# A trunk kernel: first two weight groups in pieces of 272, 384 and 448 columns, work moved between engines at the start, and another order at the end

## The reference, cut to what matters

```python
q, k, v, g, gg, pv, pg, fq, fk, fv, logf, fg = split(rmsnorm(h, norm_pre) @ w_in)   # 1024 -> 3222 columns
g = log_sigmoid(glr @ w_up + b_gate) / 16          # forget gate, from the 16 low-rank columns glr
o_gla  = chunked gated linear attention(q, k, v, g)
o_pool = (trailing means of pv - pv) @ pool_w * pool_scale
o_fox  = forgetting softmax attention(fq, fk, fv, cumsum(logf)), for the samples over the cache too
y = concat(rmsnorm(o_gla) * silu(gg), o_pool * silu(pg), o_fox * silu(fg)) @ w_out
h = h + rmsnorm(y, norm_post)
```

## Time and profile before

| what | value |
|---|---|
| median of 3 runs | 712.42 us (710.39 to 712.92) |
| the profiled execution | 712.99 us, span 711.3 us |
| TensorE busy | 667.0 us of the span (94%) |
| VectorE, ScalarE, GpSimd busy | 389.3, 256.9, 140.0 us |
| first matmul of weight group 2 | at 48.22 us |
| first matmul of the output projection | at 604.30 us |
| last matmul | at 702.97 us |

### The profile page before, as it was taken

One profiled execution on the slowest core, in us unless ns is written; L12 is line 12 of the kernel. 1 busy time (PEld: TensorE's weight loads), 2 busy tenths in 40 slices (PEclk: granted clock), 3 DMA queues, 4 the chain that ended last, 5 costly groups with the idle time before them and its releaser, 6 DMA issues.

```text
span 711.3 us, 13069 instructions
## 1 busy us (share of the span) xinstructions
PE 667.0 (94%) x5120; PEld 565.3 (79%) x5120; DVE 389.3 (55%) x706; ACT 256.9 (36%) x453; POOL 140.0 (20%) x161
## 2 busy tenths in 40 slices
PE   2999999999999999999999989999899887999995
PEld 2799999888999989999999945666576654688884
DVE  4824926572455305169999956345433549245433
ACT  6637343111111256122121154644564557221221
POOL 3034112111111011233222130223222102112210
PEclk9999999999999999999999999999999999999999
DMA  8412103131001032352210480557665502032232
GB/s 245 121 38 54 36 1 73 32 89 30 7 27 30 5 83 91 100 168 72 59 30 1 138 272 3 176 180 212 185 214 176 208 32 103 1 105 96 82 119 89
DMA packets 60758, 67.28 MB, mean 95 GB/s; under 512 B 15188, under 2 KB 50907, under 8 KB 60697
## 3 DMA queue, kind: packets, MB, share of 16 engines
q1 hardware_dynamic: 55529, 51.37, 24.4%
q0 software_dynamic: 5168, 15.08, 6.8%
HBM read 57.71 MB, written 8.68 MB: 93 GB/s over the span
## 4 chain that ended last, share of the span: by engine, by line
PE 66%; DVE 20%; issue 4%; ACT 4%; SPq 3%; DMA 2%; DVEq 0%; ACTq 0%
PE PS L1743 9%; PE PS L1744 8%; PE PS L1745 8%; DVE RA L1412 7%; PE PS L1672 5%; PE PS L1671 5%; PE PS L1673 5%; PE PS L2032 3%; PE PS L1989 3%; PE PS L1967 3%; PE PS L2014 2%; PE PS L1932 2%; PE PS L1919 2%; DVE wr L1241 2%; DVE PT L1611 1%
## 5 line engine op out<-in xcount | busy, mean ns | idle before, releaser
L1743 PE MATMUL PS<-xh,wh 128*128 128x368 f32 x576 | 196.6, 341 | 0.9 <-DVE RA L1372 0.6
L1744 PE MATMUL PS<-xl,wh 128*128 128x368 f32 x576 | 190.5, 331 | 0.0
L1745 PE MATMUL PS<-xh,wl 128*128 128x368 f32 x576 | 190.0, 330 | 0.0
L568 POOL TENSOR_TENSOR wl<-wr,wh 128x1024 fp32r<-128x1024 f32 x24 | 61.7, 2570 | 298.0 <-ACT wh L929 298.0
L1743 PEld LDWEIGHTS PS<-xh,wh 128*128 128x128 f32 x576 | 108.5, 188 | 5.2 <-issue 2.5
L1744 PEld LDWEIGHTS PS<-xl,wh 128*128 128x128 f32 x576 | 108.5, 188 | 0.9
L1745 PEld LDWEIGHTS PS<-xh,wl 128*128 128x128 f32 x576 | 108.5, 188 | 0.0
L1241 DVE TENSOR_TENSOR wr<-wr,small 128x1024 f32<-128x1024 f32 (+1 forms) x26 | 37.0, 1426 | 44.6 <-DMA wr<-in_w_in_dram 44.5
L1671 PE MATMUL PS<-woh,yh 128*128 128x512 f32 (+1 forms) x144 | 56.2, 390 | 1.7 <-DVE wol_b L1575 1.7
L1412 DVE RECIPROCAL RA<-RA 128x1104 f32<-128x1104 f32 x8 | 56.4, 7054 | 0.3
L1673 PE MATMUL PS<-woh,yl 128*128 128x512 f32 (+1 forms) x144 | 56.0, 389 | 0.0
(11 more groups left out here) (301 smaller groups left out, 1092.9 us busy)
## 6 DMA issues: line engine op xcount, KB each, us to landing
wr<-in_w_in_dram SPq DMA_DIRECT2D x24, 512.0 KB, 3.9
kpage<-in_cache_fox_k_dram SPq DMA_DIRECT2D x64, 192.0 KB, 2.7
RA<-in_cache_fox_v_dram POOLq DMA_DIRECT2D x32, 192.0 KB, 3.4
pagesB<-in_cache_fox_v_dram POOLq DMA_DIRECT2D x32, 192.0 KB, 3.5
YF<-in_x_prompt_dram SPq DMA_DIRECT2D x8, 512.0 KB, 7.0
xres<-in_x_prompt_dram SPq DMA_DIRECT2D x8, 512.0 KB, 4.0
out_y_p_dram<-zout SPq DMA_DIRECT2D x16, 256.0 KB, 2.0
wo_raw_a<-in_w_out_dram SPq DMA_DIRECT2D x6, 512.0 KB, 4.9
```

The source lines that it names most:

```text
L568: eng.tensor_tensor(low, wr[:, c % 2, :, 0:m], wh[:, c % 2, :, 0:m].bitcast(F32), ALU.subtract).then_inc(wlo_done, 1)
L1743: pe.matmul(out, high, xh[:, k, cols], start=(k == 0), stop=False)
L1744: pe.matmul(out, high, xl[:, k, cols], start=False, stop=False)
L1745: ins = pe.matmul(out, low, xh[:, k, cols], start=False, stop=(k == KT - 1))
```

## The change

**Start.** The thirds become pieces of 272, 384 and 448 columns, which end with the tiles i = 2, 5 and 8. Before each piece there are only the tiles that it needs: TensorE's order is now tiles 0 to 2, group 1 over 272 columns, tile 3, group 0 over 272, tiles 4, 5, 6, group 1 over 384, tile 7, group 0 over 384, tile 8, group 0 over 448, group 1 over 448. norm_pre comes as 8 rows and TensorE transposes it. Group 1 is loaded before group 0 and before the third prompt tile. The scaling and the low part of the groups 0 and 1 go from DVE to POOL. The tiles 4, 6 and 8 are squared on DVE instead of ACT, and scaled on POOL instead of DVE.

**End.** W and X are placed earlier in `TAIL`. The output projection signals its first half by itself; ACT squares each half when it is done; DVE multiplies by norm_post before the root is there, and joins root and sum with x in one instruction for each half.

```diff
+FIRST_COLS = [slice(0, NMETA + 2 * P), slice(NMETA + 2 * P, NMETA + 5 * P), slice(NMETA + 5 * P, NT)]
+BY_ACT, BY_DVE = [0, 1, 2, 3, 5, 7], [4, 6, 8]
...
-TAIL = {(2, 2, 1): [("W", 0)], (2, 2, 2): [("X", 0), ("W", 1)], (2, 2, 3): [("X", 1), ("W", 2), ("Y", SAMPLE)],
...
+TAIL = {(2, 2, 0): [("W", 0), ("W", 1)], (2, 2, 1): [("X", 0), ("W", 2)],
+        (2, 2, 2): [("X", 1), ("X", 2), ("W", 3)], (2, 2, 3): [("X", 3), ("W", 4), ("Y", SAMPLE)],
...
+            sp.dma_start(gpre_rows, a["norm_pre"][0].rearrange("(k p) -> k p", p=P)).then_inc(d_gpre, 16)
             for i, t in enumerate(XORDER):
                 load_x(t)
...
+                if i == 2:
+                    load_w(1)
                 if i == 3:
                     load_w(0)
-                if i == 4:
-                    load_w(1)
...
+            w_scale(g, 1)
+            w_scale(g, 0)
+            w_low(g, 1)
+            w_low(g, 0)
+            for i in BY_DVE:
+                t = XORDER[i]
+                g.wait_ge(refined, BY_DVE.index(i) + 1)
+                g.tensor_scalar(xrows[:, t, :], xrows[:, t, :], rstd[:, t:t + 1], refine[:, t:t + 1],
+                                ALU.mult, ALU.mult).then_inc(xs_pool, 1)
...
-            for i in range(1, 9, 2):
-                x_squares(i)
-                if i >= 3:
-                    x_high(i - 2)
-                x_squares(i + 1)
-                x_roots(i, 2)
...
+            x_squares(3)
+            w_high(0)
+            x_roots(3, 2)
+            x_high(3)
+            x_squares(5)
+            x_high(4)
+            x_roots(5, 2)
+            x_squares(7)
+            x_high(5)
+            x_high(6)
+            x_roots(7, 2)
+            lf_high(0)
             x_high(7)
+            x_high(8)
             lf_high(1)
-            x_high(8)
...
+                act.wait_ge(out_half, n_ + 1)
...
+                act.activation(zout[0:m, low], s_slot(user)[0:m, low], ACT.Square, accum_out=zhalf[0:m, 0:1]
+                               ).then_inc(half_squared, 1)
...
+            def x_squares(i):
...
+                dve.tensor_tensor_reduce(squares_v, xrows[:, t, :], xrows[:, t, :], 1.0, 0.0, ALU.mult, ALU.add,
+                                         ssq[:, t:t + 1]).then_inc(sqv_done, 1)
...
+                for n_half, cols in enumerate(halves):
+                    dve.wait_ge(half_squared, 2 * n_ + n_half + 1)
+                    ins = dve.tensor_tensor(zout[0:m, cols], s_slot(user)[0:m, cols], gpost[0:m, cols], ALU.mult)
...
+                for cols in halves:
+                    dve.scalar_tensor_tensor(out=zout[0:m, cols], in0=zout[0:m, cols], scalar=zstat[0:m, 1:2],
+                                             in1=xres[0:m, cols], op0=ALU.mult, op1=ALU.add).then_inc(y_done, 1)
...
+            def first_chunk(t):
...
+                for k in range(KT):
+                    pe.matmul(out, wh[:, 1, k, :], xh[:, k, cols], start=(k == 0), stop=False)
+                    if t:
+                        pe.matmul(out, wl[:, 1, k, :], xh[:, k, cols], start=False, stop=False)
+                pe.wait_ge(xlo_done, (6, 12, 18)[t])
+                for k in range(KT):
+                    ins = pe.matmul(out, wh[:, 1, k, :], xl[:, k, cols], start=False, stop=(t > 0 and k == KT - 1))
...
+                for i in range(3):
+                    x_transposes(i)
+                first_chunk(0)
+                x_transposes(3)
+                low_rank(0)
+                for i in range(4, 7):
+                    x_transposes(i)
+                first_chunk(1)
+                x_transposes(7)
+                low_rank(1)
+                x_transposes(8)
+                low_rank(2)
+                first_chunk(2)
```

More of the change, by code:

```diff
@@ L283, in build @@
         zvar = small[:, 24:25]
+        zhalf = small[:, 0:2]
         head_of = small[:, 40:44]
@@ L357, in build @@
         gate_parts = [(E[:, 0, :], E[:, 2, :]), (E[0:64 + H, 1, :], E[0:64 + H, 3, :])]
-        squares = RA[:, 3 * D:4 * D]
+        squares, squares_v = RA[:, 3 * D:4 * D], QK[:, 1, 0:D]
+        gpre_rows = QK[0:KT, 2, 0:P]
         rstd, refine = RA[:, 4 * D:4 * D + 9], RA[:, 4 * D + 9:4 * D + 18]
@@ L919, in lf_high @@
                     act.wait_ge(in_full, 1)
-                act.activation(low_h[0:64, cols], PS[0:64, 0, 0:TH], ACT.Copy).then_inc(low_high, 1)
+                act.activation(low_h[0:64, cols], PS[0:64, 0, 0:cols.stop - cols.start], ACT.Copy).then_inc(low_high, 1)
             def w_high(c):
@@ L1363, in store @@
                     dve.wait_ge(in_full, c + 1)
-                    dve.tensor_copy(thirds(Y[:, c - C_GV, :]), src).then_inc(done, 1)
+                    if c == 1:
+                        for n_, cols in enumerate(FIRST_COLS):
+                            ins = dve.tensor_copy(Y[:, 0, cols], PS[:, 3 + n_, 0:cols.stop - cols.start])
+                        ins.then_inc(done, 1)
+                    else:
+                        dve.tensor_copy(thirds(Y[:, c - C_GV, :]), src).then_inc(done, 1)
                 elif c == C_GKA:
@@ L1689, in low_rank @@
             def low_rank(t):
-                cols = slice(TH * t, TH * t + TH)
+                cols = FIRST_COLS[t]
+                m = cols.stop - cols.start
+                if t:
+                    pe.wait_ge(lf_low, t)
+                else:
+                    pe.wait_ge(whi_done, scaled_at(0))
+                    pe.wait_ge(wlo_done, scaled_at(0))
+                pe.wait_ge(xlo_done, (6, 12, 18)[t])
                 for k in range(KT):
-                    both = (PS[0:64, 0, 0:TH], wh[:, 0, k, 0:64], xh[:, k, cols])
-                    rest = (PS[0:32, 0, 0:TH], wh[:, 0, k, 0:32], xl[:, k, cols])
+                    both = (PS[0:64, 0, 0:m], wh[:, 0, k, 0:64], xh[:, k, cols])
+                    rest = (PS[0:32, 0, 0:m], wh[:, 0, k, 0:32], xl[:, k, cols])
                     if k:
@@ L1700, in low_rank @@
                 ins.then_inc(in_full if t == 2 else lf_full, 1)
-            def first_chunks():
-                rows_at = {(0, 3): 6, (0, 7): 7}
-                for t in range(3):
-                    x_low_done(pe, (3, 6, 8)[t])
-                    if t == 0:
-                        pe.wait_ge(wlo_done, 1)
-                        pe.wait_ge(whi_done, 1)
-                    else:
-                        pe.wait_ge(lf_low, t)
-                    low_rank(t)
-                    if t < 2:
-                        x_transposes((5, 8)[t])
-                    if t == 0:
-                        pe.wait_ge(wlo_done, 2)
-                        pe.wait_ge(whi_done, 2)
-                    cols = slice(TH * t, TH * t + TH)
-                    for k in range(KT):
-                        high, low = wh[:, 1, k, :], wl[:, 1, k, :]
-                        out = PS[:, 3 + t, 0:TH]
-                        pe.matmul(out, high, xh[:, k, cols], start=(k == 0), stop=False)
-                        pe.matmul(out, high, xl[:, k, cols], start=False, stop=False)
-                        ins = pe.matmul(out, low, xh[:, k, cols], start=False, stop=(k == KT - 1))
-                        if (t, k) in rows_at:
-                            x_transposes(rows_at[t, k])
-                ins.then_inc(in_full, 1)
@@ new lines, in first_chunk @@
+            def first_chunk(t):
+                cols = FIRST_COLS[t]
+                out = PS[:, 3 + t, 0:cols.stop - cols.start]
+                pe.wait_ge(xhi_done, (6, 12, 18)[t])
+                if t == 0:
+                    pe.wait_ge(whi_done, scaled_at(1))
+                for k in range(KT):
+                    pe.matmul(out, wh[:, 1, k, :], xh[:, k, cols], start=(k == 0), stop=False)
+                    if t:
+                        pe.matmul(out, wl[:, 1, k, :], xh[:, k, cols], start=False, stop=False)
+                pe.wait_ge(xlo_done, (6, 12, 18)[t])
+                for k in range(KT):
+                    ins = pe.matmul(out, wh[:, 1, k, :], xl[:, k, cols], start=False, stop=(t > 0 and k == KT - 1))
+                if t == 0:
+                    pe.wait_ge(wlo_done, scaled_at(1))
+                    for k in range(KT):
+                        ins = pe.matmul(out, wl[:, 1, k, :], xh[:, k, cols], start=False, stop=(k == KT - 1))
+                if t == 2:
+                    ins.then_inc(in_full, 1)
@@ L1904, in side @@
                 ins.then_inc(ring_full, 1)
-            for i in range(5):
-                x_transposes(i)
             first_chunks()
@@ L2061, in project_out @@
                                   lambda k: (woh[:, k, cols], wol[k][:, cols]))
-                ins.then_inc(s_full, 1)
+                    ins.then_inc((out_half, s_full)[half], 1)
             for key in SIDE[NCHUNK - 1]:
```

166 lines of the change are left out of this document (93 added, 73 removed).

## The result

| | time in us |
|---|---|
| forecast | 715.5 (709.3 to 719.5) |
| changed kernel, median of 22 runs | 713.61 (710.67 to 716.20) |
| kernel before, median of 22 runs beside them | 711.88 (708.76 to 714.90) |
| ratio | 1.0030, 95% interval 1.0017 to 1.0043 |
| profiled execution after | 714.7, span 713.0 (before: 712.99, span 711.3) |

A forecast was written before the change was run, and what follows sets the result against it. TensorE, busy 667.0 of 711.3 us, was taken as the bound. 712.99 + 6.1 (start) - 1.35 (w_out slices) - 1.7 (last tile) gave 716.0 us profiled, 715.5 for the runs, range 709.3 to 719.5.

The forecast's parts named there:

- The start: Up to group 2's first matmul: new TensorE pauses and lower clock outweigh dense work beginning earlier; +6.1 us.
- walk of +7.1: Step-by-step timing of the start's queues, putting group 2's first matmul at 55.3 us, 7.1 us behind 48.2.
- The pauses: TensorE without work behind tile 4's transposes, 3.0 us, and before group 0's piece of 448 columns, 2.0 us.
- the 1.8 us in group 1's first piece: TensorE waits 1.8 us in group 1's 272-column piece for tile 2's low part on DVE, ending at 19.7.
- the 0.4 us for POOL's scaling of tile 6: At the start, POOL's scaling of tile 6, taken as 1.3 us behind DVE's of tile 5, adds 0.4 us waiting.
- The blocks: At the start, two-input DVE instructions wait out POOL's SBUF-reading ones; tile 2 is scaled 1.5 us later.
- rival 3: POOL bounds the start: its scaling of tiles 4, 6 and 8 exceeds 1.7 us; 718.5 us, chance 0.20.
- TAIL: End of the attention stage: earlier w_out slices start the projection at 602.95 instead of 604.30; -1.35 us.
- it starts by 599.2, held by POOL's block for most of that time: DVE's copy near the attention stage's end, previously at 599.6, has one low part ahead instead of two.
- Last tile: Behind the last matmul: halved squares and norm_post's product beside the root shorten the end; -1.7 us.
- Rival 1: Blocks and lower clock cost little, the start ends where it did; 709.3 us, chance 0.20.
- rival 2: TensorE is fed from 16.2 us on without new pauses, so the start is faster; 706.5 us, chance 0.10.

The follow-up runs named there:

- e2_start: The kernel before with the changed start alone, its TAIL and last tile left as before; ratio 1.0104 to the kernel before, 717.77 us beside 711.24.
- e4_no_wscale: The changed kernel without POOL's scaling of weight groups 0 and 1 by norm_pre, load still waited for; ratio 1.0026 to the kernel before, 713.19 us.
- e5_fed: The changed kernel with the start's work reordered on ACT, DVE and TensorE, same instructions; ratio 0.9925 to the kernel before, 706.62 us beside 712.32.
- e7_halves: The kernel before with only the last tile's squaring and finishing by halves; ratio 0.9974 to the kernel before, 710.79 us beside 712.32.

## Why the prediction was right, and where not

**The start.** Right in its mechanism and nearly in its size: +6.75 us in the trace for a forecast of +6.1 and a walk of +7.1; +7.4 (4.8 to 10.0) by the runs of e2_start. That the single trace came so near has luck in it: the same start began group 2 at 51.52 and 53.41 us in two other executions, 3.3 and 5.2 us later than before. The change's whole effect is 2.1 us, smaller than that spread. The pauses came as walked (3.09 for 3.0, 2.03 for 2.0). Two smaller ones did not: the 1.8 us in group 1's first piece were 0 here, 0.43 or 0.44 in most of the other traces and 2.16 in e4_no_wscale, and of the 0.4 us for POOL's scaling of tile 6 at most 0.2 are there (in e2_start 16 transposes take 2.08 us, where 16 without a wait take 1.91). The landing of group 1 was put at 10.0 and was 11.8 (12.6 in e5_fed), which moved the piece from 16.2 to 17.6; that is where the 1.8 us went, since tile 2's low part no longer came late. The clock rose at about 22 us, not 25.5: in the rows of 21.5 to 22.0 us four matmuls begin in half a microsecond, in the next half six. These errors nearly cancel.

**What the walk could not give** is one number for the clock: the same pauses give 51.5 to 55.0 us for group 2. The first trace after had the lowest granted clock of them (0.84).

**The blocks.** DVE's tiny instruction under POOL's scaling of group 1 took 1.39 us (1.77 in e2_start), and 0.22 in every trace in which POOL's product began behind it; then tile 2's scaling was held instead (2.09 to 2.44, and 0.81 without POOL's product). Tile 4's squares took 2.26 us against 1.22. The rule from the Trainium skill ("SBUF — State Buffer", section "Who interferes with whom"), that such instructions of DVE and POOL block each other, agrees for these. It blocks in both directions, and only the DVE side was walked. POOL's scaling of a tile took 1.73 us, and 2.79 for tile 4, more than the 1.7 us at which rival 3 was to decide. But each time it starts 0.06 or 0.07 us behind a scaling on DVE, and it ends 0.9 to 1.0 us behind the last of DVE's instructions in that place (the scaling of 28.88, the squares of 20.91). So its own time is some 1.0 us (an estimate from these ends; no run shows it alone), and the rest is waiting, which the walk had counted already. TensorE waited for it by 0.2 us at most.

**TAIL.** The step that failed in size: "it starts by 599.2, held by POOL's block for most of that time". Less the shift of 5.93 us at 584 us, the last large copy of the changed kernel starts at 598.2 (604.12), 1.3 us before the 599.54 of the kernel before, not 0.34. The low part ahead of it was not held by POOL; it started first, and POOL was held. DVE then waited 1.32 us for TensorE's transposes ahead of that copy, so DVE no longer set its time. The 1.13 us behind the copy came as worked out. In sum -2.5 for -1.35, within the bounds given (+0.3 to -3.2).

**Last tile.** -1.7 us, as worked out; e7_halves gives 1.9 (0.6 to 3.1), and the eight tiles before cost nothing.

**Sum.** 716.0 was expected of the profiled execution, which has 714.7: 1.1 us from TAIL, 0.8 us in the stages between, against 0.65 us more at the start. Rival 1 falls by group 2's start, rival 2 by the pauses, rival 3 because TensorE waited for POOL's scaling by 0.2 us at most. The sign within the bound, and the direction, were right because a loss of 6 to 7 us stood against a gain of 3 to 4.

## What to carry to other kernels

Where several engines share a pipeline, walk the queues of all of them between two things that TensorE waits for: here a new order of TensorE's work, with the emptying of group 0's bank moved to suit it, left the pauses nearly as they were (e3_order, no gain), and taking one scaling out from behind a low part on DVE removed 2.4 us of pause (e8_ahead, 3 to 4 us). A change that is neutral in sum can be a gain and a loss: its end alone was worth 3.9 us, its start cost 7.4, and both together with the start's queues in another order were 5.3 us faster than before. Of these 5.3 the end gives most; that the new start is worth anything by itself these runs don't show.

## What was not expected of the hardware

- Behind a pause the lower clock can follow, and not always for as long. Behind a pause of 3.09 us the same 16 transposes took 3.67, 3.33 and 2.08 us in three executions, with a granted clock over 24 to 56 us of 0.84, 0.95 and 1.00.
- The block of DVE and POOL fell on whichever started second: DVE 2.25 and 3.98 us for one and two low parts of 1.21 before, POOL 3.27 instead of 2.37 after. The single one of before (POOL, then DVE):

```profile
592.24 1.27 POOL L876 TENSOR_TENSOR yl<-YF,yh 128x512 fp32r<-128x512 f32 x1 [36.46 <-ACT yh L1148]
592.34 2.25 DVE L1575 TENSOR_TENSOR wol_a<-wo_raw_a,woh 128x1024 fp32r<-128x1024 f32 x1
```

- As the rows of 20.18 to 20.91 us read, a POOL instruction that waited was passed by the next one on DVE as well: behind DVE's scaling at 20.18 came the squares at 20.91, at their full speed (1.22), and POOL's scaling of 20.25 took 2.79 us. A DVE instruction with a single input (reciprocal, 0.16 us) was not held in the same place where the next, with two inputs and a scalar, took 1.39.
- POOL's product of 128x1024 with a vector broadcast along the inner dimension took 1.90 us (e5_fed) where its subtraction of two full inputs takes 2.36 to 2.40.
